# Three squares summed on VectorE, half of the ones matmuls, and two weight remainders moved to GpSimd

## The reference

```python
h = rmsnorm(x, norm_pre[l, s]) * (1.0 + scale) + shift
f = sublayer(h)                                     # mixer (s = 0) or conv_ffn (s = 1)
x = x + gate * rmsnorm(f, norm_post[l, s])

def rmsnorm(x, g):
    return x * lax.rsqrt(jnp.mean(x * x, axis=-1) + EPS) * g
```

## Time and profile before

| | us |
|---|---|
| median of 3 runs | 1924.89 |
| lowest, highest run | 1924.59, 1927.86 |
| profiled execution: span from first to last instruction | 1928.5 |
| PE busy | 1839.8 |
| DVE busy | 964.3 |
| ACT busy | 827.8 |
| POOL busy | 55.0 |

### The profile page before, as it was taken

How to read it: one execution, slowest core, us unless ns; L and a number is a source line. 1 busy time by engine, 2 the same in 40 slices (tenths; PEclk the granted TensorE clock), 3 DMA queues, 4 the chain that set the end, 5 groups by cost and what they waited for, 6 DMA issues and landing times.

```text
span 1928.5 us, 36407 instructions
## 1 busy us (share of the span) xinstructions
PE 1839.8 (95%) x14838; PEld 1698.7 (88%) x14838; DVE 964.3 (50%) x1613; ACT 827.8 (43%) x1420; POOL 55.0 (3%) x76
## 2 busy tenths in 40 slices
PE   6999989988899999999999999999999999999998
PEld 3999866667799999999999897776899999999997
DVE  4433355556746655235555743344375553255555
ACT  4545422225745544124445653343465441244453
POOL 0000222220000000000000000000000000000000
PEclk9999999999999999999999999999999999999999
DMA  7222377651021223222234311111211222122243
GB/s 284 67 62 61 111 222 227 218 158 56 1 71 45 76 70 88 71 66 68 73 95 139 95 44 29 29 31 31 67 44 55 76 84 80 55 76 76 78 135 115
DMA packets 244483, 170.24 MB, mean 88 GB/s; under 512 B 20778, under 2 KB 230924, under 8 KB 243212
## 3 DMA queue, kind: packets, MB, share of 16 engines
q1 hardware_dynamic: 244364, 168.55, 29.2%
HBM read 165.08 MB, written 3.44 MB: 87 GB/s over the span
## 4 chain that ended last, share of the span: by engine, by line
PE 83%; DVE 6%; ACT 4%; DMA 4%; issue 3%; SPq 0%; ACTq 0%; DVEq 0%
PE ps L2015 46%; PE ps L2091 15%; PE ps L2048 4%; DMA w_mod_raw<-in_w_mod 3%; PE ps L2209 2%; PE ps L2722 2%; PE ps L2759 2%; PE ps L2718 2%; PE ps L2408 1%; PE ps L2228 1%; PE ps L2590 1%; PE ps L2461 1%; PE ps L2567 1%; ACT w_hi L790 1%; PE ps L2036 1%
## 5 line engine op out<-in xcount | busy, mean ns | idle before, releaser
L790 ACT ACTIVATE w_hi<-w_raw 128x1024 fp32r<-128x1024 f32 (+4 forms) x187 | 198.6, 1062 | 560.8 <-PE ps L2015 436.1
L1374 DVE TENSOR_TENSOR w_lo<-w_raw,w_hi 128x1024 fp32r<-128x1024 f32 (+4 forms) x191 | 234.2, 1227 | 377.2 <-ACT w_hi L790 376.7
L2015 PE MATMUL ps<-h_hi,w_hi 128*128 128x322 f32 x1648 | 381.5, 313 | 3.2 <-ACT conv L980 1.7
L2015 PE MATMUL ps<-h_lo,w_hi 128*128 128x322 f32 x1648 | 380.2, 312 | 0.0
L2015 PE MATMUL ps<-h_hi,w_lo 128*128 128x322 f32 x1648 | 378.1, 310 | 0.0
L2015 PEld LDWEIGHTS ps<-h_hi,w_hi 128*128 128x128 f32 x1648 | 278.1, 189 | 4.8 <-ACT conv L1200 2.0
L2015 PEld LDWEIGHTS ps<-h_lo,w_hi 128*128 128x128 f32 x1648 | 279.1, 189 | 0.0
L2015 PEld LDWEIGHTS ps<-h_hi,w_lo 128*128 128x128 f32 x1648 | 279.1, 189 | 0.0
L2091 PE MATMUL ps<-g_hi,w_hi 128*128 128x322 f32 x352 | 110.7, 314 | 2.7 <-DVE g_lo L1858 1.6
L2091 PE MATMUL ps<-g_lo,w_hi 128*128 128x322 f32 x352 | 109.6, 311 | 0.0
L2091 PE MATMUL ps<-g_hi,w_lo 128*128 128x322 f32 x352 | 109.1, 310 | 0.0
(11 more groups left out here) (376 smaller groups left out, 3339.2 us busy)
## 6 DMA issues: line engine op xcount, KB each, us to landing
w_raw<-in_ffn_w_up SPq DMA_DIRECT2D x88, 512.0 KB, 3.7
w_mod_raw<-in_w_mod SPq DMA_DIRECT2D x80, 512.0 KB, 4.6
w_raw<-in_ffn_w_down SPq DMA_DIRECT2D x48, 704.0 KB, 4.4
w_raw<-in_ev_w_in SPq DMA_DIRECT2D x18, 512.0 KB, 3.7
w_mod_first<-in_w_mod SPq DMA_DIRECT2D x8, 1024.0 KB, 15.7
w_raw<-in_ev_w_out SPq DMA_DIRECT2D x8, 512.0 KB, 4.1
w_raw<-in_od_w_out SPq DMA_DIRECT2D x8, 512.0 KB, 3.9
w_raw<-in_od_w_kv_up SPq DMA_DIRECT2D x24, 128.0 KB, 2.3
```

The lines of the kernel that those rows point to most:

```text
L790: act.activation(WH[slot][:, 0:k, :], RAW[slot][:, 0:k, :], ACT.Copy).then_inc(w_hi, 1)
L1374: dve.tensor_tensor(WL[slot][:, 0:k, :], RAW[slot][:, 0:k, :], WH[slot][:, 0:k, :].bitcast(F32), ALU.subtract).then_inc(w_lo, 1)
L2015: last = pe.matmul(out, w_of(k, wi), x_of(k, xi, i), start=(k == 0 and p == 0), stop=(k == ks - 1 and p == 2))
```

## The change

In the second half of each of the three passages:

1. Squares. VectorE adds the first three pairs of squares (two additions, `x_sum(i, 1, 1)` and `x_sum(i, 2, 1)`), the third coming from a new buffer `x_sq_again`; square 3 goes to `x_sq1`. `second_stat` has two matmuls over `x_sq1` and two over `x_sq0`, four in place of eight.
2. Place on PE. `second_stat` stands inside `second_pair(0)`, after the first of the eight steps of block u = 3, in place of before `second_pair(0)`.
3. Ahead weights. Their rests are made by GpSimd (`ahead_rest`), each waiting for the counts of `w_lo` and `w_hi`; VectorE only waits for the count behind its chunks. ScalarE makes the high part of ahead weight 3 right behind that of weight 2, before the squares.
4. For i = 1 the context turn goes to bank 5, behind a wait for the post root, and PE waits for ScalarE's copies before `second_pair(1)` in place of before `second_pair(0)`.

```diff
+    SQXA = place("x_sq_again", [2, HW], R_T)
...
+            def ahead_rest(i):
+
+                for u in (2, 3):
+                    n = N0_OUT[i] + (2 * KD if i % 2 else KD) + u
+                    w = next_weights(i, u)
+                    pool.wait_ge(w_lo, n)
+                    pool.wait_ge(w_hi, n + 1)
+                    pool.tensor_tensor(w[1][:, :, :], RAW[n % 2][:, 0:KD, :], w[0][:, :, :].bitcast(F32), ALU.subtract).then_inc(w_lo, 1)
+
...
+            ahead_rest(0)
             ffn(0)
+            ahead_rest(1)
+            ahead_rest(2)
             ffn(1)
...
                 act.wait_ge(S("x_added"), 4 * (2 * i + g) + j + 1)
                 if g == 0 and j >= 2:
-                    act.wait_ge(S("x_summed"), 3 * i + j - 1)
-                if g == 1 and j >= 2:
-                    act.wait_ge(S("x_stat"), 5 * i + j)
-                dst = SQX[j % 2] if g else SQX[min(j, 1)]
+                    act.wait_ge(S("x_summed"), 5 * i + j - 1)
+                if g == 1 and j == 3:
+                    act.wait_ge(S("x_summed"), 5 * i + 4)
+                dst = SQXA if g and j == 2 else SQX[min(j, 1)]
...
                 root(i, "post", 1)
                 ahead_hi(i, 2)
+                ahead_hi(i, 3)
                 for j in range(4):
                     x_square(i, 1, j)
-                    if j == 1:
-                        if between:
-                            between()
-                        ahead_hi(i, 3)
+                    if j == 1 and between:
+                        between()
...
-                for u in (2, 3):
-                    n = N0_OUT[i] + (2 * KD if i % 2 else KD) + u
-                    w = next_weights(i, u)
-                    dve.wait_ge(w_hi, n + 1)
-                    dve.tensor_tensor(w[1][:, :, :], RAW[n % 2][:, 0:KD, :], w[0][:, :, :].bitcast(F32), ALU.subtract).then_inc(w_lo, 1)
+                x_sum(i, 1, 1)
+                x_sum(i, 2, 1)
...
+                dve.wait_ge(w_lo, N0_OUT[i] + (2 * KD if i % 2 else KD) + 4)
...
             def second_stat(i):
 
-                for j in range(4):
-                    pe.wait_ge(S("x_squared"), 8 * i + 4 + j + 1)
-                    for x in range(2):
-                        last = pe.matmul(bank(7, HW), ONES, SQX[j % 2][:, x, :], start=(j == 0 and x == 0), stop=(j == 3 and x == 1))
-                    last.then_inc(S("x_stat"), 1)
+                pe.wait_ge(S("x_squared"), 8 * i + 8)
+                for x in range(2):
+                    pe.matmul(bank(7, HW), ONES, SQX[1][:, x, :], start=(x == 0), stop=False)
+                pe.wait_ge(S("x_summed"), 5 * i + 5)
+                for x in range(2):
+                    last = pe.matmul(bank(7, HW), ONES, SQX[0][:, x, :], start=False, stop=(x == 1))
+                last.then_inc(S("x_stat"), 1)
...
-                second_stat(i)
-                if between:
-                    pe.wait_ge(S("c_ctx"), 2)
...
                             last = half_mm(bank(4 + 2 * ((n + u) % 2) + g, HW), next_weights(i, u), (Hh, Hl), k, g, KD)
+                            if g == 0 and (u, k) == (3, 0):
+                                second_stat(i)
...
+                if between:
+                    pe.wait_ge(S("c_ctx"), 2)
                 second_pair(1)
...
+                pe.wait_ge(*root_ready(1, "post", 1))
                 for k in range(2):
-                    turn(hb(6, k), CROW[:, k, :])
-                turn(hb(6, 2), KROW[:, :]).then_inc(S("c_ctx_turned"), 1)
+                    turn(hb(5, k), CROW[:, k, :])
+                turn(hb(5, 2), KROW[:, :]).then_inc(S("c_ctx_turned"), 1)
```

More of the change, by code:

```diff
@@ L844, in root @@
                 else:
-                    act.wait_ge(S("x_stat"), 5 * i + 1 + 4 * g)
+                    act.wait_ge(S("x_stat"), 2 * i + 1 + g)
                     if g or i:
@@ L1261, in context @@
                 act.wait_ge(S("c_ctx_turned"), 1)
-                act.activation(CKV[:, :, 0:PAST], bank(6, 256).rearrange("p (k c) -> p k c", c=P), ACT.Copy).then_inc(S("c_ctx"), 1)
-                act.activation(KPT[:, 0:PAST], PS[:, 6 * 512 + 256:6 * 512 + 384], ACT.Copy).then_inc(S("c_ctx"), 1)
+                act.activation(CKV[:, :, 0:PAST], bank(5, 256).rearrange("p (k c) -> p k c", c=P), ACT.Copy).then_inc(S("c_ctx"), 1)
+                act.activation(KPT[:, 0:PAST], PS[:, 5 * 512 + 256:5 * 512 + 384], ACT.Copy).then_inc(S("c_ctx"), 1)
             second_half(1, context)
@@ L1409, in x_pair, with x_sum @@
                 dve.tensor_tensor(both_k(X, j, g), both_k(X, j, g), both_k(F, j, g), ALU.add).then_inc(S("x_added"), 1)
-            def x_sum(i, j):
-                dve.wait_ge(S("x_squared"), 8 * i + j + 1)
+            def x_sum(i, j, g=0):
+                dve.wait_ge(S("x_squared"), 8 * i + 4 * g + j + 1)
                 if j >= 2:
-                    dve.wait_ge(S("x_summed"), 3 * i + j - 1)
-                dve.tensor_tensor(SQX[0][:, :, :], SQX[0][:, :, :], SQX[1][:, :, :], ALU.add).then_inc(S("x_summed"), 1)
+                    dve.wait_ge(S("x_summed"), 5 * i + 3 * g + j - 1)
+                dve.tensor_tensor(SQX[0][:, :, :], SQX[0][:, :, :], (SQXA if g and j == 2 else SQX[1])[:, :, :], ALU.add
+                                  ).then_inc(S("x_summed"), 1)
             def h_scale(i, j):
@@ L2073, in first_stat @@
             def first_stat(i):
-                pe.wait_ge(S("x_summed"), 3 * i + 3)
+                pe.wait_ge(S("x_summed"), 5 * i + 3)
                 for x in range(2):
```

## The result

The changed kernel took 1942.17 us (median of 5 runs, 1939.22 to 1943.07) against 1927.14 us for the kernel before in the same comparison (5 runs, 1924.59 to 1930.15): 1.0077 times as long, 95% interval 1.0063 to 1.0091. The forecast was 1937.5 us, within 1926 to 1943, with a chance of 0.82 for slower. It was worked out from a median of 1924.89 us for the kernel before (3 runs); the 5 runs of this comparison put that at 1927.14, which is 2.25 of the 4.7 us between forecast and measured. The changed kernel's profiled execution took 1942.26 us with a span of 1940.5 us, 12.0 us above the 1928.5 of before (forecast: 1941.1).

What follows compares the result with a forecast made beforehand. TensorE, busy 1839.8 of 1928.5 us, was taken as the bound. Shorter statistics -3.8, contention 3 x 4.1, less 1.0, gave +7.5 us; with 5.1 for the clock +12.6, on 1924.9: 1937.5 us, range 1926 to 1943.

Steps and rivals of the forecast that it cites:

- It isn't quite: Second halves: TensorE is not quite the bound; later statistics delay the chunks, leaving -3.8 us of the matmuls' 7.2 us.
- X: Time when VectorE ends a second half's last residual add; 607.85 us for i = 0 in the kernel before.
- E: Time when TensorE ends the `L2048` chunk work and `second_pair(1)` starts; its shift is the span's shift.
- The rest parts on GpSimd: Second halves: two GpSimd subtractions stop VectorE's two-input residual instructions, 2.06 us each, 4.1 us per half.
- D: Delay of the last residual add per half from two GpSimd subtractions: 2 x 2.06 = 4.1 us.
- Stalls of 4.3, 3.1 and 4.3 us: TensorE's predicted idle times waiting for square 3 before the ones matmuls, for i = 0, 1 and 2.
- the 1.0 us: Taken off the sum for the part of i = 1's stall that TensorE's own late arrival at 1097.14 hides.
- The clock: Behind each of three new TensorE stalls the granted clock falls, slowing the ones matmuls: 5.1 us in all.
- Sum: Whole kernel: -3.8 + 3 x 4.1 less 1.0 = +7.5 us, with the clock loss +12.6, so 1937.5 us.
- only one of the two: Rival: one of a half's two subtractions stops VectorE, the first fitting a gap; 1926.3 or 1928.0 us; chance 0.09.
- the engines don't disturb each other: Rival: no contention between GpSimd and VectorE on these larger tiles, so -3.8 us stands, 1921.1 us; chance 0.13.
- VectorE keeps GpSimd out: Rival: GpSimd waits until VectorE's residual row ends, TensorE stands 5.7 us; +16.7 us, 1941.6 us; chance 0.12.

Runs made afterwards that it cites:

- the kernel that only fills: Changed kernel with GpSimd filling the six ahead rests with zeros instead of subtracting, so it reads nothing: 1924.77 us, ratio 0.9983 to the kernel before.
- the repeat: The changed kernel run again unedited beside other follow-up kernels: 1940.78 us, ratio 1.0062 to the kernel before.
- the kernel with the busy TensorE: Changed kernel with eight dummy matmuls ahead of the ones matmuls' wait, keeping TensorE at work in the stall: 1938.8 us, ratio 1.0050 to the kernel before.
- the first experiment: Changed kernel with GpSimd writing zeros into the six ahead rests in place of subtracting: 1924.77 us, ratio 0.9983 to the kernel before.
- the last kernel: Changed kernel with rests back on VectorE between its other work, square 3 in its own buffer, statistics one step earlier: 1923.08 us, ratio 0.9972 to before.
- the probe: Kernel before, plus two GpSimd subtractions, a copy and a fill of 128x1024 behind the last `h_lo` of i = 0 and 2: 1930.19 us, one run.
- four subtractions: Changed kernel with each of the six GpSimd subtractions done twice, so four per half: 1953.95 us, ratio 1.0124 to the kernel before.
- the interleaved kernel: Changed kernel with rests on VectorE (behind the first residual pair, behind the sums), a fourth square buffer, earlier statistics: 1923.08 us, ratio 0.9972 to before.

## Why the prediction was right

Term by term, forecast beside measured, in the order of the prediction:

- *"It isn't quite": the longer chain leaves -3.8 us of the 7.2.* Measured without contention -4.2 (the kernel that only fills). Root at X + 4.1: 4.10. i = 0 and 2 gave -0.98 and -1.02 (forecast -1.16 and -1.2), i = 1 -2.22 (-1.4), since the chain didn't wait there for a late TensorE (root at X + 4.10 too, against 5.07 in the forecast). The chunks do set E, as the wait of 0.21 us at 621.48 shows.
- *"The rest parts on GpSimd": D = 4.1 us.* Measured 4.28 (X at A + 10.78 and 10.79 against 6.50 and 6.51). The 2.2 us for a subtraction was low, and so was the estimate of 2.25; it is 2.39. What stopped the residual instructions was forecast from one record of 821 ns, and the 0.14 us that the stop ends ahead of GpSimd's record came out too: 604.84 - 0.82 = 604.02 against 604.15, the end of the first subtraction, and 607.78 - 0.83 = 606.95 against 607.09.
- *The rule of the Trainium skill* ("SBUF — State Buffer", "Who interferes with whom") that a VectorE instruction with two SBUF inputs contends with a GpSimd one that reads SBUF, and not with one that only writes, is borne out in both halves: 3.03 us beside the subtraction, 0.82 us beside the fill. The half that no row of before showed, VectorE's running instruction holding up GpSimd, shows here in the 0.49 us a record. But VectorE went on before GpSimd's record had ended: two whole subtractions would be a D of 4.78 us, and it was 4.28.
- *Stalls of 4.3, 3.1 and 4.3 us.* Measured 4.13, 4.14 and 4.13. The 3.1, and with it the 1.0 us that was taken off the sum for i = 1, did not come. It was read from TensorE's late arrival at the statistics of i = 1 in the kernel before, 5.06 us behind A against 3.77 for i = 0. That was the fall of the clock at 1084 us in that execution and not the place itself. Behind the same idle time the changed kernel's clock stayed up:

```profile
1088.10 0.78 PE L2081 MATMUL ps<-f_sq_sum,consts 128*128 128x322 f32 x2 [2.22 <-ACT f_sq L841]
...
1087.90:1091.90 4.00, 3.80 (x22) 3.46 (x23) 2.52 (x3) 3.90 (x10) 0.00 (x0) 1.00 0.41 114
```
  In the repeat, where it did fall near there (0.74 over 1087 to 1091), the stall of i = 1 was 3.15 us, as forecast, but A to E was no longer (27.36), since TensorE was going to wait for the squares anyway: a clock loss ahead of a stall is free. The 1.0 us does not stand alone, though. The same late arrival made the forecast gain of i = 1 too small (-1.4 for -2.22), so the two errors of i = 1 leave 0.2 us: under contention the root waits for the squares, late TensorE or not.
- *"The clock": 5.1 us.* 1.68, 1.67 and 1.21 by the kernel with the busy TensorE, 4.6. The ground for it was thinner than it looked. The second idle time of the earlier trace rows ends at 239.07 and its window at 240.00, so that row doesn't show what came behind; the trace does (1.00 over 239 to 243 us). But in six of the ten profiled executions here the clock did fall at that place, behind or within an idle time of 1.98 to 2.62 us.
- *Sum.* +8.6 without the clock (forecast 7.5). The difference is +1.0 for the term of i = 1, +0.5 for D and -0.4 for the chain. With the clock it is +13.2 (forecast 12.6), since the clock was 0.5 less. Half by half the misses without the clock are alike, 3.3, 2.1 and 3.3 us against 2.9, 1.7 and 2.9. That the sums with the clock agree within 0.6 us is in part luck: D was 0.5 too small and the clock 0.5 too large, and the fall in the kernel before makes the 13.2 smaller by about 1.2. The timed ratio is 14.8 us (12.1 to 17.5) on 1927.14. The measured 1942.17 us lies above the likeliest case's own range (1929 to 1940) and 0.8 us below the end of the whole one.

Of the rivals, *only one of the two* is refuted by the pair of long records in all three halves, *the engines don't disturb each other* by the first experiment against the changed kernel, and *VectorE keeps GpSimd out* by the ends of GpSimd's two records, 604.15 and 607.09, of which the second lies 3.9 us ahead of X.

Open: why TensorE's clock falls behind some idle times and not behind others of the same length; and whether the timed gain of the last kernel beyond -3.3 us is real. How often the kernel before has the fall at 1084 us, and so how much of the loss it hides in the timed runs, is open too: both profiled executions of its code there (the probe's is the other) had it.

## What to carry to other kernels

Before work is handed to an idle GpSimd, look at what VectorE does in that stretch: if it adds or multiplies two SBUF tiles, a GpSimd instruction that reads SBUF (here a subtraction of two tiles) can stop it for nearly its whole length. Here a 1.2 us job on VectorE became a 2.4 us one on GpSimd that cost VectorE 2.1. Ask what waits on the delayed row too; here a TensorE idle of 4.1 us also cost the fast clock just where the short critical chain needed it. And when a rhythm differs in one of three equal places of the profile, check the granted clock there before building a term of the sum on it.

## What was unexpected of the hardware

- The two engines took turns strictly, one instruction each: VectorE's addition (to 601.89), GpSimd's subtraction (its 2.39 us of work ending at 604.15), VectorE's product (604.84), GpSimd's second one (607.09), VectorE's addition (607.78). In these traces neither got two in a row while both had one ready, with four subtractions too. Each engine has a short gap or wait between its instructions, so whether the other one simply gets in there, or turns are dealt out, is not shown. GpSimd began about 0.14 us before VectorE's record ended (607.09 - 2.39 = 604.70 against 604.84), the same lead as the other way round.
- The recorded duration holds the wait: 2.88 us for 2.39 of work on GpSimd, 3.03 for 0.82 on VectorE. Neither shows as idle time.
- The same idle time of 2.22 us at the same place left TensorE's clock at 0.57 over the 4 us behind it in the kernel before and at 1.00 in the changed kernel. It stands there in all ten profiled executions, and in four of them the clock fell (the kernel before, the probe, the busy TensorE and the repeat). Those of 4.13 us brought 0.50 each time, as did all eighteen of 2.9 to 5.9 us in the changed stretches of these kernels, and those of 0.93, 1.22 and 0.93 us in the interleaved kernel left it at 1.00.
